# Stick-breaking attention beside HGRN2 on one core: the sum over later keys carried as one row, value products in pairs, a fourth score bank

## The chip, the cores and the metric

One core of a Trainium2 chip runs the whole kernel. The metric is the device time of one execution in microseconds (us). In the rows and in the text the engines are PE (TensorE), DVE (VectorE), ACT (ScalarE), POOL (GpSimd) and SP (SyncE, which issues most transfers). PEld is TensorE's weight load.

## What is computed

One layer of a streaming encoder, for 1024 prompt positions and 8 streams of 16 new positions, all in fp32. After a norm, one projection feeds branch A (stick-breaking attention, 8 heads of 64), branch B (HGRN2, 4 heads of 128) and two merge gates. The change touches branch A's prompt attention:

```python
def stick_breaking_block(q, k, v, q_pos, k_pos):
    z = jnp.einsum('bthd,bshd->bhts', q, k) * (SB_HEAD_DIM ** -0.5)
    mask = k_pos[None, :] < q_pos[:, None]
    log_fail = jnp.where(mask, jax.nn.log_sigmoid(-z), 0.0)
    after = lax.cumsum(log_fail, axis=3, reverse=True) - log_fail
    a = jnp.where(mask, jnp.exp(jax.nn.log_sigmoid(z) + after), 0.0)
    return jnp.einsum('bhts,bshd->bthd', a, v)
...
y = x + rms_norm((merged @ w_out), g_post)
```

With sp = softplus(z), the weight of key s for query t is exp(z - sum of sp over all keys from s up to t). So each key tile needs, besides its own triangle, the sum of sp over all later keys.

## The kernel before

The order of every engine is written out by hand, with semaphores between them. After a prologue (norm, first projections) the program runs four times, once for each pair of heads `p`, an **attention stage** of 27 steps (`B_STEPS`) and then a **recurrence stage** (`A_STEPS`) for HGRN2. Into both stages pieces of eight matmuls of the input projection (`product`, L623) are spread by `B_PIECES` and `A_PIECES`. Then come gates and branch products (L909), the output projection and a tail that normalises and stores y.

An attention step `n` stands for one tile of 128 keys against a window of 512 queries of one head. `STEPS` runs over two windows `wd`, over the key tiles `j` from the last to the first, and over the two heads `h`; `tile_rank(n)` counts the key tiles from the last, and diagonal tiles use only the columns from `first_col(n)` (128, 256, 384 or 512 columns are left). In step n each engine does, in this order:

- PE: the scores of step n into `Z[n % 3]` (L685, L686; the queries split into a high and a low part), pieces of the projection, then for step n-2 the accumulation on the scores (`add`, L699): `negtri` times the softplus's high part SPH and low part SPL, and `negones` times the later-key sum's high part SUH and low part SUL (for the second key tile the fp32 `SUM`, as one fp32 matmul). Then more pieces, and the value product of step n-3 (L739): `v_nat` with 128 columns (both heads' values) against `Aw`, into one bank per head, `OH = (OB, XB)`; half of each result is used.
- ACT: exponential (L1116) and log (L1118) of the scores, together the softplus; the exponential of step n-2's log weights into `Aw` (L1126); evacuations of projection windows (`window_recurrence`, `forget`).
- DVE: the maximum that guards the softplus (L1370), on diagonal tiles the causal product (L1374), SPH and SPL (L1381, L1383), SUH and SUL (L1389, L1391); scans of the forget gate, and the split of the next weight chunk (`split_weights`, L1244, L1246).
- POOL: the causal product on `Aw` (L1678) and the running sum `SUM[h]` (`later_sum`, L1660 to L1670).

The high and low parts are fp32r (a matmul on them is one pass, one on fp32 takes two records). In the tail (L1614, L1619) DVE scales rows 0 to 5 of y and adds the residual, and POOL does rows 6 and 7 (`finish`, L1724, L1726), for each of three windows.

## Time and profile before

| what | us |
|---|---|
| median of 3 runs | 1159.33 (1159.21 to 1160.43) |
| profiled execution | 1159.81 |
| its span, first to last instruction | 1158.0 |
| TensorE busy | 1109.8 |
| VectorE busy | 739.9 |
| ScalarE busy | 466.6 |
| GpSimd busy | 278.6 |

The mean granted clock of TensorE was 0.991 of full speed. Busy times are unions of the records of an engine. A matmul's record is longer than the time that it keeps the array from the next one, since matmuls are pipelined; the distance between the starts of two neighbours tells the second. The attention stages run from 88.5 to 175.8 us, 263.2 to 350.5, 438.0 to 525.3 and 612.7 to 700.0; the recurrence stages lie between them and the last after them.

### The profile page before, as it was taken

The numbers are of one execution on the slowest core, as the hardware profiler recorded it, in microseconds if no ns is written. First come the engines' busy times: TensorE is split into PE (matmuls) and PEld (weight loads), VectorE is DVE, ScalarE is ACT, GpSimd is POOL, SyncE is SP. The second block draws the span as 40 slices with busy tenths as digits, with TensorE's granted clock in tenths as the row PEclk, the third lists the DMA queues.
The fourth block names the chain that finished last, engine by engine and source line by source line (L and its number), as shares of the span: only waits on it lengthen the run. The fifth ranks groups of instructions, "written<-read, shape, count | busy, mean of one in ns | idle before, by whom it ended". The sixth has DMA issues, their size and how long they took to land.

```text
span 1158.0 us, 17212 instructions
## 1 busy us (share of the span) xinstructions
PE 1109.8 (96%) x6486; PEld 1039.7 (90%) x6486; DVE 739.9 (64%) x1347; ACT 466.6 (40%) x923; POOL 278.6 (24%) x306
## 2 busy tenths in 40 slices
PE   3999999999999999999999999999999999999994
PEld 2899988999988999988999987999999999999993
DVE  7747986787986787986787995764332312352228
ACT  4345544155544155543146545346022232242221
POOL 2113422213422213422114422110211100121225
PEclk9999999999999999999999999999999999999997
DMA  6023021115021115021115021205111111111144
GB/s 241 19 71 117 19 91 55 39 46 164 19 92 55 40 39 171 20 91 55 39 40 171 19 91 55 101 19 179 56 37 37 54 39 37 43 49 37 38 182 163
DMA packets 41458, 84.89 MB, mean 73 GB/s; under 512 B 2080, under 2 KB 22176, under 8 KB 41248
## 3 DMA queue, kind: packets, MB, share of 16 engines
q1 hardware_dynamic: 40800, 81.43, 21.6%
q10 hardware_dynamic: 576, 2.36, 0.6%
q8 instruction: 52, 0.85, 0.3%
q14 instruction: 30, 0.25, 0.1%
HBM read 67.27 MB, written 16.52 MB: 72 GB/s over the span
## 4 chain that ended last, share of the span: by engine, by line
PE 88%; DVE 6%; ACT 2%; DMA 1%; issue 1%; SPq 0%; DVEq 0%; ACTq 0%
PE bank L623 56%; PE bank L909 9%; PE bank L699 5%; PE bank L739 5%; PE bank L832 2%; PE bank L855 2%; PE bank L686 2%; PE bank L685 2%; DVE xw L1344 1%; DVE imaskL L1303 1%; DVE yb L1614 1%; PE bank L873 1%; PE bank L783 1%; PE bank L761 1%; DVE St L1530 1%
## 5 line engine op out<-in xcount | busy, mean ns | idle before, releaser
L623 PE MATMUL bank<-xl,wh 128*128 128x384 f32 x1344 | 459.0, 342 | 6.7 <-DVE xl L1340 6.7
L623 PE MATMUL bank<-xh,wh 128*128 128x384 f32 x1344 | 454.9, 338 | 4.3 <-ACT xh L1090 3.5
L623 PE MATMUL bank<-xh,wl 128*128 128x384 f32 x1344 | 456.7, 340 | 0.0
L623 PEld LDWEIGHTS bank<-xl,wh 128*128 128x128 f32 x1344 | 253.5, 189 | 14.3 <-DVE xl L1340 8.1
L623 PEld LDWEIGHTS bank<-xh,wh 128*128 128x128 f32 x1344 | 253.8, 189 | 13.5 <-issue 10.6
L623 PEld LDWEIGHTS bank<-xh,wl 128*128 128x128 f32 x1344 | 253.9, 189 | 7.9 <-issue 4.2
L1244 DVE CAST wh<-wr 128x1024 fp32r<-128x1024 f32 x64 | 51.1, 798 | 102.3 <-PE bank L623 102.3
L1034 ACT ACTIVATE slot<-bank,ngate 128x384 f32<-128x384 f32 x48 | 27.7, 578 | 190.7 <-PE bank L623 188.0
L1701 POOL TENSOR_TENSOR imaskH<-i_nat,k 128x512 fp32r<-128x512 f32 (+1 forms) x36 | 50.5, 1407 | 188.1 <-PE bank L832 188.1
L1246 DVE TENSOR_TENSOR wl<-wr,wh 128x1024 fp32r<-128x1024 f32 x64 | 93.1, 1454 | 2.2
L1713 POOL TENSOR_TENSOR slot<-slot,slot 128x384 f32<-128x384 f32 x24 | 32.7, 1364 | 241.0 <-DVE slot L1579 240.8
L1116 ACT ACTIVATE E<-bank 128x512 f32<-128x512 f32 (+3 forms) x96 | 46.9, 489 | 96.6 <-PE bank L686 96.4
L739 PE MATMUL bank<-Aw,v_nat 128*128 128x512 f32 (+3 forms) x192 | 77.4, 484 | 0.0
L1578 DVE TENSOR_TENSOR slot<-bank,slot 128x384 f32<-128x384 f32 x24 | 13.4, 557 | 100.2 <-PE bank L909 100.2
L1670 POOL TENSOR_TENSOR SUM<-SUM,E 128x512 f32<-128x512 f32 (+3 forms) x64 | 60.2, 941 | 60.5 <-DVE SUL L1391 43.8
L1370 DVE SCALAR_TENSOR_TENSOR E<-E,bank 128x512 f32<-128x512 f32 (+3 forms) x96 | 52.6, 548 | 33.9 <-ACT E L1118 33.8
L909 PE MATMUL bank<-gl,wh 128*128 128x384 f32 x192 | 65.0, 339 | 0.0
L909 PE MATMUL bank<-gh,wh 128*128 128x384 f32 x192 | 65.0, 339 | 0.0
L909 PE MATMUL bank<-gh,wl 128*128 128x384 f32 x192 | 65.0, 339 | 0.0
L1126 ACT ACTIVATE Aw<-bank 128x512 f32<-128x512 f32 (+3 forms) x96 | 46.2, 481 | 42.3 <-PE bank L699 42.3
L1530 DVE SCALAR_TENSOR_TENSOR St<-St,gg,bank 128x128 f32<-128x128 f32 x128 | 44.3, 346 | 23.6 <-PE bank L855 15.8
L1303 DVE SCALAR_TENSOR_TENSOR imaskL<-i_nat,k,imaskH 128x128 fp32r<-128x128 f32 x160 | 53.5, 397 | 0.0
(193 smaller groups left out, 1749.1 us busy)
## 6 DMA issues: line engine op xcount, KB each, us to landing
wr<-wch SPq DMA_DIRECT2D x64, 512.0 KB, 3.7
KTc<-ckT SPq DMA_DIRECT2D x4, 2048.0 KB, 8.9
Vc<-cv SPq DMA_DIRECT2D x4, 2048.0 KB, 8.3
xw<-xT SPq DMA_DIRECT2D x6, 768.0 KB, 10.1
graw<-gated SPq DMA_DIRECT2D x8, 576.0 KB, 5.8
xres<-xT SPq DMA_DIRECT2D x1, 4608.0 KB, 16.6
yT<-yb SPq DMA_DIRECT2D x6, 576.0 KB, 3.0
okT<-kT ACTq DMA_DIRECT2D x4, 576.0 KB, 3.0
```

The source lines that it names most:

```text
L623: i = nc.tensor.matmul(CH[n % 2][:, 0:WIN], weights[:, k, :], rows[:, k, w * WIN:(w + 1) * WIN], start=(m == 0), stop=(m == 23))
L699: return nc.tensor.matmul(Z[m % 3][:, lo:QW], weights, rows[:, lo:QW], start=False, stop=True, skip_group_check=True)
L739: nc.tensor.matmul(OH[h][:, c0:QW], v_nat[:, j * P:(j + 1) * P], Aw[m % 2][:, c0:QW], start=(j == 4 * wd + 3), stop=(j == 0), skip_group_c ...
L909: i = nc.tensor.matmul(bk[:, 0:WIN], weights[:, t, :], rows[:, ROW_OF[t], w * WIN:(w + 1) * WIN], start=(m == 0), stop=(m == 11))
L1116: nc.scalar.activation(E[n % 3][:, c0:QW], Z[n % 3][:, c0:QW], ACT.Exp).then_inc(s_E, 1)
L1244: V.tensor_copy(wh[g % 2][:, :, :], wr[g % 3][:, :, :]).then_inc(s_whi, 1)
L1246: V.tensor_tensor(wl[g % 3][:, :, :], wr[g % 3][:, :, :], wh[g % 2][:, :, :].bitcast(F32), ALU.subtract).then_inc(s_wlo, 1)
L1303: i = V.scalar_tensor_tensor(imaskL[:, b0 + b, :], i_nat[:, c * P:(c + 1) * P], rows[:, b:b + 1], imaskH[:, b0 + b, :].bitcast(F32), ALU.m ...
L1370: i = V.scalar_tensor_tensor(e[:, c0:QW], e[:, c0:QW], 88.0, Z[n % 3][:, c0:QW], ALU.min, ALU.max)
L1530: V.scalar_tensor_tensor(St[(n + 1) % 8][:, :], St[n % 8][:, :], gg[:, n:n + 1], Z[b % 2][:, s * P:(s + 1) * P], ALU.mult, ALU.add).then_i ...
L1670: G.tensor_tensor(dst[:, lo:QW], dst[:, lo:QW], src[:, lo:QW], ALU.add).then_inc(s_S, 1)
L1701: G.tensor_tensor(imaskH[:, b0:b0 + blocks, :], i_nat[:, None, c * P:(c + 1) * P].broadcast_to([P, blocks, P]), rows[:, :, None].broadcast ...
```

## The change

1. **Later-key sums as one row.** `SUM`, `SUH`, `SUL` and POOL's `later_sum` go. Row 0 of the finished log weights of a tile less row 0 of its scores is minus the sum of softplus over that tile and all later keys. ACT copies row 0 of the scores to `zr`; after the accumulation DVE subtracts (`later_row`), ACT writes the high part to row 0 of `RT[h]`, and DVE the low part to row 32 (`later_row_low`). One matmul with `rows_r` (ones in rows 0 and 32) spreads both.
2. **Paired value products.** In every even step PE multiplies the tiles of both heads, each with its own 64 columns of `v_nat`, into partitions 0 to 63 and 64 to 127 of the one bank `OB`.
3. **Fourth score bank.** The bank that is freed joins the score banks (`ZB`). `E` has two buffers and not three, `Aw` three and not two.
4. **High parts by ScalarE.** SPH is written by ACT, after DVE's maximum and before DVE's low part.
5. **Tail.** DVE does all eight rows of y, in three groups for each window; POOL's `finish` goes.

```diff
+def row_col(n):
+    return min(first_col(n), QW // 2)
...
-                        need(pe, s_a, t - 2)
+                        need(pe, s_a, t - 3)
+                        if n >= 4:
+                            need(pe, s_S, SUMS * p + sums_until(n - 4))
...
-                            if q == 1:
-                                pe.wait_ge(s_S, SUMS * p + sums_until(m - 2))
-                                add(negones, SUM[h], cs)
-                            else:
-                                pe.wait_ge(s_Sh, SUM_SPLITS * p + sum_rows_until(m))
-                                add(negones_r[:, :], SUH[h], cs)
-                                pe.wait_ge(s_Sl, SUM_SPLITS * p + sum_rows_until(m))
-                                add(negones_r[:, :], SUL[h], cs)
+                            pe.wait_ge(s_Sl, SUMS * p + sums_until(m - 2))
+                            add(rows_r[:, :], RT[h], row_col(m - 2))
...
-                        nc.tensor.matmul(OH[h][:, c0:QW], v_nat[:, j * P:(j + 1) * P], Aw[m % 2][:, c0:QW],
-                                         start=(j == 4 * wd + 3), stop=(j == 0), skip_group_check=True).then_inc(s_av, 1)
+                        for h in range(2):
+                            r = slice(DH * h, DH * h + DH)
+                            nc.tensor.matmul(OB[r, c0:QW], v_nat[:, j * P + DH * h:j * P + DH * h + DH],
+                                             Aw[(n - 4 + h) % 3][:, c0:QW], start=(j == 4 * wd + 3), stop=(j == 0),
+                                             skip_group_check=True).then_inc(s_av, 1)
...
+                        if STEPS[n][1] > 0:
+                            need(act, s_Sl, SUMS * p + (sums_until(n - 4) if n >= 4 else 0))
+                            nc.scalar.activation(zr[n % 4][0:1, row_col(n):QW], ZB[n % 4][0:1, row_col(n):QW], ACT.Copy)
...
+                    if n < NS and tile_rank(n) > 0:
+                        c0, t = first_col(n), NS * p + n
+                        act.wait_ge(s_sp, t + 1)
+                        nc.scalar.activation(SPH[n % 2][:, c0:QW], E[n % 2][:, c0:QW], ACT.Copy).then_inc(s_sph, 1)
+                    if 2 <= n <= NS + 1 and STEPS[n - 2][1] > 0:
+                        m, cols = n - 2, slice(row_col(n - 2), QW)
+                        act.wait_ge(s_rz, 2 * (p + 1))
+                        act.wait_ge(s_S, SUMS * p + sums_until(m))
+                        nc.scalar.activation(RT[STEPS[m][2]][0:1, cols], zr[m % 4][0:1, cols], ACT.Copy).then_inc(s_Sh, 1)
...
+            def later_row(p, m):
+                cols = slice(row_col(m), QW)
+                row = zr[m % 4][0:1, cols]
+                dve.wait_ge(s_a, NS * p + m + 1)
+                V.tensor_tensor(row, ZB[m % 4][0:1, cols], row, ALU.subtract).then_inc(s_S, 1)
+
+            def later_row_low(p, m):
+                h, cols = STEPS[m][2], slice(row_col(m), QW)
+                dve.wait_ge(s_Sh, SUMS * p + sums_until(m))
+                V.tensor_tensor(RT[h][32:33, cols], zr[m % 4][0:1, cols], RT[h][0:1, cols].bitcast(F32),
+                                ALU.subtract).then_inc(s_Sl, 1)
```

How the order changes. First PE, first attention stage, around a value product of a full-width step. `bank4` holds the scores of step n-2, `k2` and `negtri_r` are constants. Before:

```order
L739 MATMUL bank7<-Aw1_116,v_nat_68 128x512
L685 MATMUL bank3<-QS1_88,KS1_86 128x512
L686 MATMUL bank3<-QL1_81,KS1_86 128x512
L699 MATMUL bank4<-SPH1_106,negtri_r_96 128x512
L699 MATMUL bank4<-SUH1_112,negones_r_97 128x512
L699 MATMUL bank4<-SUL1_114,negones_r_97 128x512
L699 MATMUL bank4<-SPL1_108,negtri_r_96 128x512
```

Now:

```order
L733 MATMUL bank5<-Aw2_116,v_nat_68 64x512
L733 MATMUL bank5<-Aw0_114,v_nat_68 64x512
L689 MATMUL bank7<-QS1_88,KS1_86 128x512
L690 MATMUL bank7<-QL1_81,KS1_86 128x512
L703 MATMUL bank3<-SPH1_105,negtri_r_96 128x512
L703 MATMUL bank3<-RT1_109,rows_r_97 128x512
L703 MATMUL bank3<-SPL1_107,negtri_r_96 128x512
```

Two products of 64 output columns stand in a row, in every second step, where one of 128 stood in each; four accumulations are three.

ACT in one full-width step of the same stage (`bank4` and `bank2` are the scores, `zr` and `RT` the rows). Before:

```order
L1116 ACTIVATE E1_103<-bank3 128x512
L1118 ACTIVATE E1_103<-E1_103 128x512
L1126 ACTIVATE Aw0_115<-bank4 128x512
L944 ACTIVATE tmpT0_94<-bank0 128x384
L1116 ACTIVATE E2_104<-bank4 128x512
```

Now:

```order
L1113 ACTIVATE E0_102<-bank4 128x512
L1116 ACTIVATE zr2_112<-bank4 1x512
L1118 ACTIVATE E0_102<-E0_102 128x512
L1126 ACTIVATE Aw1_115<-bank2 128x512
L1130 ACTIVATE SPH0_104<-E0_102 128x512
L1135 ACTIVATE RT0_108<-zr0_110 1x512
L939 ACTIVATE tmpT1_95<-bank1 128x384
L1113 ACTIVATE E1_103<-bank7 128x512
```

Three instructions of a step are six, and the window's evacuation stands behind the two that wait for DVE.

DVE in the same place. Before:

```order
L1370 SCALAR_TENSOR_TENSOR E0_102<-E0_102,bank2 128x512
L1381 CAST SPH0_105<-E0_102 128x512
L1383 TENSOR_TENSOR SPL0_107<-E0_102,SPH0_105 128x512
L1389 CAST SUH0_111<-SUM0_109 128x512
L1391 TENSOR_TENSOR SUL0_113<-SUM0_109,SUH0_111 128x512
L1423 SCALAR_TENSOR_TENSOR lf_74<-k2_89,lf_74 128x128
```

Now, with the split of a weight chunk behind it:

```order
L1399 SCALAR_TENSOR_TENSOR E0_102<-E0_102,bank4 128x512
L1312 TENSOR_TENSOR zr0_110<-bank2,zr0_110 1x512
L1411 TENSOR_TENSOR SPL0_106<-E0_102,SPH0_104 128x512
L1318 TENSOR_TENSOR RT0_108<-zr0_110,RT0_108 1x512
L1442 SCALAR_TENSOR_TENSOR lf_74<-k2_89,lf_74 128x128
L1253 CAST wh0_57<-wr2_55 128x1024
L1255 TENSOR_TENSOR wl2_56<-wr2_55,wh0_57 128x1024
L1399 SCALAR_TENSOR_TENSOR E1_103<-E1_103,bank7 128x512
```

The casts left DVE; two instructions on one row came in their place, each between two of ACT's.

## Rows read from the trace of the kernel before

**Rows 1.** The page's busy times, and the chain that ended last, by line.

```profile
PE 1109.8 (96%) x6486; PEld 1039.7 (90%) x6486; DVE 739.9 (64%) x1347; ACT 466.6 (40%) x923; POOL 278.6 (24%) x306
...
by line: PE bank L623 55.8%; PE bank L909 8.8%; PE bank L699 5.5%; PE bank L739 5.4%; PE bank L832 2.1%; PE bank L855 1.8%; PE bank L686 1.5%; PE bank L685 1.5%; issue 1.3%; DVE xw L1344 1.2%; DVE imaskL L1303 1.1%; DVE yb L1614 0.7%; PE ba
```

**Rows 2.** Windows of attention stages: length; busy PE, PEld, DVE, ACT, POOL; clock; DMA.

```profile
263.20:350.50 87.30, 87.30 (x462) 77.06 (x464) 72.59 (x145) 46.36 (x97) 29.58 (x48) 1.00 0.27 81
...
sum 349.20, PE 349.20 PEld 308.26 DVE 290.26 ACT 185.48 POOL 118.23; mean PE 87.30 PEld 77.06 DVE 72.57 ACT 46.37 POOL 29.56
```

**Rows 3.** Groups by form, PE, whole span: line, operands, count, busy us, mean ns.

```profile
L699 PE MATMUL bank<-SUL,negones_r 128*128 128x512 f32 x32 | 12.7, 397 | 0.0
...
L761 PE MATMUL bank<-KTc,qbd 128*32 128x512 f32 x64 | 7.7, 598 | 0.0
...
L699 PE MATMUL bank<-SUM,k 128*128 128x128 f32 x32 | 6.1, 274 | 0.0
...
L699 PE MATMUL bank<-SUL,negones_r 128*128 128x384 f32 x16 | 5.4, 340 | 0.0
...
L699 PE MATMUL bank<-SUL,negones_r 128*128 128x256 f32 x16 | 4.4, 278 | 0.0
```

**Rows 4.** Timeline, PE, a full-width step: start us, duration us, line, operands.

```profile
333.29 0.40 PE L699 MATMUL bank<-SUH,negones_r 128*128 128x512 f32 x1
333.52 0.40 PE L699 MATMUL bank<-SUL,negones_r 128*128 128x512 f32 x1
```

**Rows 5.** Timeline, PE, end of the second attention stage: the sample scores.

```profile
349.91 0.61 PE L756 MATMUL bank<-kTs,qbd 128*128 128x128 f32 x4
350.45 1.92 PE L761 MATMUL bank<-KTc,qbd 128*32 128x512 f32 x16
352.30 0.44 PE L623 MATMUL bank<-xh,wh 128*128 128x384 f32 x1
352.58 0.34 PE L623 MATMUL bank<-xl,wh 128*128 128x384 f32 x1
```

**Rows 6.** Timeline, ACT, a full-width step; idle before and its releaser in brackets.

```profile
331.86 0.60 ACT L1116 ACTIVATE E<-bank 128x512 f32<-128x512 f32 x1 [2.24 <-PE bank L686]
332.49 0.63 ACT L1118 ACTIVATE E<-E 128x512 f32<-128x512 f32 x1
334.19 0.60 ACT L1126 ACTIVATE Aw<-bank 128x512 f32<-128x512 f32 x1 [1.07 <-PE bank L699]
334.69 0.49 ACT L959 ACTIVATE tmpT<-bank 128x384 f32<-128x384 f32 x1
335.06 0.50 ACT L944 ACTIVATE zB<-bank 128x384 f32<-128x384 f32 x1
```

**Rows 7.** Groups by form, ACT: copies of other shapes (last row: stage of 264:351).

```profile
L997 ACT ACTIVATE QS<-qT 64x1024 fp32r<-64x1024 f32 x16 | 16.9, 1059 | 0.4
...
L1056 ACT ACTIVATE gh<-graw 128x1152 fp32r<-128x1152 f32 x8 | 9.2, 1156 | 3.3 <-DMA graw<-gated 3.3
...
L1116 ACT ACTIVATE E<-bank 128x256 f32<-128x256 f32 x4 | 1.5, 384 | 3.9 <-PE bank L686 3.9
```

**Rows 8.** Timeline, DVE: a weight split before a maximum; the causal product (ns min/median/max).

```profile
336.73 1.46 DVE L1244 CAST wh<-wr 128x1024 fp32r<-128x1024 f32 x1
338.22 1.23 DVE L1246 TENSOR_TENSOR wl<-wr,wh 128x1024 fp32r<-128x1024 f32 x1
339.37 0.68 DVE L1370 SCALAR_TENSOR_TENSOR E<-E,bank 128x512 f32<-128x512 f32 x1
...
L1374 DVE TENSOR_TENSOR E<-E,k x64: 291/336/907, 86.6 to 654.2; 128x128 f32<-128x128 f32 x64
```

**Rows 9.** Timeline, the tail: second and third window on DVE, POOL and ACT.

```profile
1136.55 1.36 DVE L1614 TENSOR_TENSOR yb<-yb,yrs 128x1152 f32<-128x1152 f32 x1 [1.09 <-ACT yrs L1220]
1136.60 3.00 POOL L1724 TENSOR_TENSOR yb<-yb,yrs 128x768 f32<-128x768 f32 x1 [0.26 <-ACT yrs L1220]
1137.94 2.87 DVE L1619 TENSOR_TENSOR yb<-yb,xres 128x1152 f32<-128x1152 f32 x1
...
1142.14 0.52 ACT L1220 ACTIVATE yrs<-yrs 128x384 f32<-128x384 f32 x1
...
1152.14 1.36 DVE L1619 TENSOR_TENSOR yb<-yb,xres 128x1152 f32<-128x1152 f32 x1
```

177 lines of the change are left out of this document (67 added, 110 removed).

## The prediction

> **What bounds the kernel now.** I began with the chain that ended last and the busy times of the page [rows 1]. The chain is TensorE for 88% of the span, and its two attention lines are 5.4% (L739, the value products) and 5.5% (L699, the accumulations on the scores). So what TensorE no longer does comes off the end, as long as no other engine is late. Then I cut the span into the four attention stages, one for each pair of heads [rows 2]. Each takes 87.3 us, and TensorE is busy for the whole of it; VectorE has 72.6 us of work in it, ScalarE 46.4 and GpSimd 29.6. Beyond these stages the edit touches only the last 20 us, where the output is scaled and the residual is added [rows 9]. The recurrence stages, the gates and the output projection keep their instructions.
>
> **What TensorE loses.** (1) *Later-key sums.* Each of the 64 SUL matmuls goes. In the timeline one of 512 columns follows the next after 0.23 us [rows 4]; with 0.17 for 384 and 0.115 for 256 columns, in proportion, 32, 16 and 16 of them [rows 3] are 7.4 + 2.8 + 1.8 = 12.0 us. The SUH matmul stays as one with RT, with the same columns. The 16 fp32 SUM matmuls of 128 columns are 32 records. A record's duration is its stream and about 0.17 of pipeline (a 512-column one shows 0.40 and is followed after 0.23), so one streams for 0.11, in all 3.4 us. In their place come 16 matmuls of 256 columns at 0.115, 1.8 us. Net 13.6 us over four stages, 3.4 each.
>
> (2) *Value products.* L739 holds 5.4% of 1158.0 us, 62.5 us [rows 1]. Now two products of 64 output columns each, one for each half of the array, stand where two of 128 stood. Does the array run both at once? The sample scores (L761) are the nearest row: products of 32 output columns with 512-column fp32 streams. A record shows 0.60 [rows 3], a stream of 0.43, and 16 of them are done in 1.92 us [rows 5]; one after the other they would take 6.9, so four ran at a time. I take two at a time here: 31.3 us remain.
>
> The same rows show a price. L756's last record ends at 350.52, so its stream ended 0.17 earlier, at 350.35, and L761 is first seen at 350.45. The second of the full-array matmuls behind starts at 352.58; less one spacing of 0.17 the first took effect at 352.41. Between 350.35 and 352.41 lie 2.06 us, and four rounds of 0.43 fill 1.71 of them. So one excursion into divided columns costs 0.35 us. The change makes one every second step, 12 per stage and 48 in all: 16.8 us. Value products then cost 31.3 + 16.8 = 48.1 us and save 14.4, which is 3.6 per stage and not 7.8. The bounds are 0 (the gap at L761 is its weight loads and hides here) and 0.5 us per excursion.
>
> The Trainium skill (TensorEngine Tiling (Array Packing), Key Properties) says that changing the tiling mode drains TensorE; the rows agree. The same skill's tensor-engine page (TensorE: Matmul & The Clock Gate, Measured speedup vs the span model) gives a packed group one matmul's duration and about 4 ns per tile, with no term for the drain; by it alone the sum would be 16.8 us lower.
>
> Together a stage of TensorE's work shrinks from 87.3 to 87.3 - 3.4 - 3.6 = **80.3 us**.
>
> **What the other engines get.** *ScalarE.* Per stage it takes over 20 high parts of the softplus (12 of 512 columns, 4 of 384, 4 of 256), and gets 20 one-row copies zr and 20 one-row copies RT (8 of 512, 4 of 384, 8 of 256 each). One row has no precedent in the trace. The nearest are the copies on 64 partitions, 1.06 us for 1024 columns, beside 1.16 for 1152 on all 128 [rows 7]: the columns count, not the partitions. I take the full price; the lower bound is the cost of a short instruction, half of it. An instruction that waits for nothing follows the last one after 0.50 us at 512 columns and 0.37 at 384 [rows 6], and 0.28 at 256 (0.38 less the same overlap of 0.10) [rows 7]. High parts: 6.0 + 1.5 + 1.1 = 8.6. Each kind of row copy: 4.0 + 1.5 + 2.2 = 7.7. ScalarE: 46.4 + 8.6 + 15.4 = 70.4 us.
>
> It also waits inside the step now, since the high part stands behind VectorE's maximum. That takes 0.68 [rows 8] from the log's end, of which the weights' exponential hides about 0.5: 0.2 us, 20 times. On the 12 diagonal steps with a high part the causal product adds 0.29 [rows 8]. That is 4.0 + 3.5, so ScalarE's own pace is near **78 us per stage**, 2.3 under TensorE's. Queued behind its two new waits are the next step's exponential and the window evacuations, and TensorE waits for both.
>
> *VectorE.* It loses 20 SPH, 16 SUH and 16 SUL instructions per stage and gets 20 + 20 row instructions: much the same total, so I cost it at nothing. The cover is that VectorE is busy for 72.6 us of a stage that still lasts over 80. *GpSimd* loses its sums (L1660 to L1670), and VectorE loses whatever sharing with them costs it.
>
> *Stalls.* The two paces lie close, and the work isn't even. In steps with a 512-column row ScalarE needs about 0.5 + 0.5 + 0.5 + 0.5 for its first four instructions, 0.2 of waiting, and 0.5 + 0.5 for high part and row: 3.3 to 3.5 us. Window work comes on top (30 instructions of about 0.5 in 27 steps, 0.6 per step): 4.1 us. TensorE's mean for such a step is two passes of scores, three accumulations (5 x 0.23), 1.5 pieces of eight at 0.17 (2.1), and half a value pair (0.6): 3.85. Over ten such steps ScalarE falls 2 to 3 us behind. The accumulation of step n comes two steps after its scores, and the fourth score bank lets TensorE run ahead, so about one step (4 us) of lag is hidden. I charge 1.5 us of stall per stage, between 0 and 4. The fourth bank and the third Aw buffer themselves cost nothing.
>
> *The tail.* In the last stage the VectorE instructions take 1.36 us alone and 2.9 beside GpSimd's [rows 9]. Afterwards GpSimd has none and VectorE has six per window: 4 x 1.36 + 2 x 0.91 = 7.3 us. From 1136.55 two windows end at 1151.2, and the third window's rstd (1142.66) is ready before. Before, the last instruction ended at 1153.50. Gain **2.3 us** (1.5 to 3). In the prologue two small fills replace a cast, at most 0.2 us, left out.
>
> **The sum.** 4 x (7.0 - 1.5) = 22.0, and 2.3 at the tail: 24.3 us. The profiled execution took 1159.8 (span 1158.0), 0.5 above the median, which I leave inside the rounding: 1159.8 - 24.3 = **1135.5 us**.
>
> **Rivals.**
> - *A, the exchange between ScalarE and VectorE sets the pace.* For: 46.4 becomes 78 against 80.3, and every step now passes ScalarE, VectorE, ScalarE, VectorE twice. Against: ScalarE idles 2.24 us before a step's first exponential now [rows 6]. If each of 24 steps takes 0.25 us more than I gave it, the stage is 84: 1159.8 - 13.2 - 2.3 = 1144.3 us; with 0.33, 86 and 1152.3.
> - *B, the excursion is free.* TensorE would need 76.1 us per stage, and then ScalarE's 78 sets it: 1159.8 - 37.2 - 2.3 = 1120.3 us. Against it stands the gap in [rows 5]. By the tensor-engine page's rule TensorE would get there, and ScalarE would still hold it at this time.
> - *C, the two halves run one after the other.* Value products 62.5 + 16.8: the stage is 87.3 - 3.4 + 4.2 = 88.1, and the time 1159.8 + 3.2 - 2.3 = 1160.7, no change. Against: four at a time in [rows 5].
> - *D, slower: the weight split blocks the exchange.* In VectorE's queue the split of the next chunk (1.46 + 1.23, 2.7 us) stands ahead of the next step's maximum [rows 8], behind which ScalarE's high part now waits. There are four per stage, 10.8 us. If all of it is exposed on top of 78, the stage is 88.8 and the time 1159.8 + 6.0 - 2.3 = 1163.5. It is slower from 9.9 us exposed (a stage over 87.9). Against: ScalarE's first three instructions of the step, 1.6 us, run beside it, and the lag of a step hides more.
> - *E, it doesn't do what it says:* if rows of one partition went at half price ScalarE would have slack, and my stalls would be 0: 1129.5, inside the forecast.
>
> **Chances.** Forecast (1127 to 1141) 0.51; A (1141 to 1156) 0.21; B (1116 to 1127) 0.13; C 0.05; D 0.10. The range 1120 to 1152 takes in nearly all of A and B; C, D and 0.04 of their outer ends are left out. Faster by over 0.2% (under 1157, about what a measurement of this kernel can tell from no change) 0.85, within 0.2% 0.05, slower 0.10.
>
> **What would show it.** The attention stages: about 82 us each, with TensorE at 80 busy. The spacing at the value pair: two records at a time, and a 0.35 us gap around them; no gap is B, four records in a row is C. The one-row copies at 0.6 us for 512 columns. ScalarE near 71 us busy per stage, its idle before the high part ended by VectorE, and TensorE's idle before L703 ended by VectorE's low parts: 1.5 us per stage is the forecast, over 3 is A, and if it follows weight splits D. Tail: no VectorE instruction over 1.4 us once GpSimd is done. I am wrong if TensorE's work per stage isn't within 79 to 82, or if stalls exceed 4 us.

## The result

| | median us | runs | ratio to before, 95% interval |
|---|---|---|---|
| before | 1159.88 | 1159.21 to 1160.60 | 1 |
| after | 1151.29 | 1150.96 to 1152.38 | 0.9927 [0.9910, 0.9945] |

The change makes the kernel faster by 8.6 us, 0.7%. The forecast was 24.3. The profiled execution has a span of 1150.6 us. Its page, first the busy times and then the chain that ended last, by engine and by line:

```profile
PE 1092.2 (95%) x6406; PEld 1003.2 (87%) x6406; DVE 717.0 (62%) x1307; ACT 556.1 (48%) x1163; POOL 188.6 (16%) x180
...
PE 73%; DVE 12%; ACT 10%; issue 3%; DMA 1%; SPq 0%; ACTq 0%; DVEq 0%
PE bank L621 48%; PE bank L904 9%; DVE E L1399 3%; PE bank L703 2%; PE bank L827 2%; ACT E L1118 2%; PE bank L733 2%; ACT SPH L1130 2%; PE bank L850 2%; ACT E L1113 2%; DVE E L1403 1%; DVE xw L1371 1%; DVE imaskL L1326 1%; PE bank L689 1%; ACT RT L1135 1%
```

Against [rows 1] the chain has left TensorE: its share was 88% and is 73%. In its place stand VectorE's maximum and causal product (L1399, L1403) and ScalarE's exponential, logarithm, high part and row copy (L1113, L1118, L1130, L1135). These are the links of one step's exchange.

The windows of the attention stages, with the columns of [rows 2]:

```profile
262.00:348.60 86.60, 83.32 (x440) 68.29 (x442) 67.73 (x131) 68.75 (x157) 11.46 (x18) 0.98 0.25 82
610.00:696.50 86.50, 82.74 (x444) 67.15 (x446) 67.75 (x131) 68.95 (x158) 11.76 (x19) 1.00 0.26 83
sum 345.60, PE 331.79 PEld 271.04 DVE 270.92 ACT 274.81 POOL 46.08; mean PE 82.95 PEld 67.76 DVE 67.73 ACT 68.70 POOL 11.52
```

TensorE is no longer busy for the whole of a window. Counted from the first score matmul to the first sample score (the **stage length** from here on; the windows above begin about 5 us later), a stage takes 89.98, 90.82, 90.88 and 90.35 us; it took 91.5 before. So a stage gave back about 1 us, not 5.5. What TensorE waited for between 88 and 697 us, the three longest in total (us in total, times, longest):

```profile
PE bank L631 <- ACT tmpT L939: 9.9, 6, 2.3
PE bank L763 <- DVE Es L1304: 4.5, 6, 1.2
PE bank L689 <- DVE zr L1312: 2.4, 8, 0.4
```

And what ScalarE and VectorE waited for there:

```profile
ACT SPH L1130 <- DVE E L1403: 35.3, 48, 0.9
...
ACT SPH L1130 <- DVE E L1399: 19.0, 32, 1.4
...
DVE E L1399 <- ACT E L1118: 45.7, 60, 1.3
...
DVE SPL L1411 <- ACT SPH L1130: 10.5, 48, 0.3
```

L763 waits at the start of the sample attention and did so before. The other two are new. The longest waits are those of the transposes (L631) for an evacuation of a projection window (`tmpT`), which stands in ScalarE's queue behind the high part and the row copy. For the row itself (L703, for VectorE's low part) TensorE waited 0.6 us in all, where the forecast had looked for the stalls.

Where the lag comes from is seen in ScalarE's timeline of step 14, one of the last diagonal steps (start us, duration, line; in brackets the idle time before it and who ended it):

```profile
126.15 0.57 ACT L1113 ACTIVATE E<-bank 128x512 f32<-128x512 f32 x1
126.62 0.57 ACT L1116 ACTIVATE zr<-bank 1x512 f32<-1x512 f32 x1
127.10 0.61 ACT L1118 ACTIVATE E<-E 128x512 f32<-128x512 f32 x1
127.62 0.47 ACT L1126 ACTIVATE Aw<-bank 128x384 f32<-128x384 f32 x1
128.81 0.63 ACT L1130 ACTIVATE SPH<-E 128x512 fp32r<-128x512 f32 x1 [0.72 <-DVE E L1403]
129.34 0.51 ACT L1135 ACTIVATE RT<-zr 1x384 fp32r<-1x384 f32 x1
129.76 0.47 ACT L1004 ACTIVATE kb<-bank 128x384 f32<-128x384 f32 x1
130.13 0.57 ACT L1113 ACTIVATE E<-bank 128x512 f32<-128x512 f32 x1
```

Apart from the 0.72 us in which VectorE takes the maximum and the causal product, ScalarE has no gap: the step takes it 3.98 us. TensorE is quicker there. Its scores of step 12 start at 116.67 us and ScalarE's exponential of them at 118.58; for step 16 it is 129.38 and 135.36. So over four steps TensorE went on by 3.2 us a step and ScalarE by 4.2, and its distance grew from 1.9 to 6.0 us. Two of these four steps, 12 and 15, also hold the three instructions of the forget gate (1.6 us together), so the gate's work is clumped just where TensorE's steps are short. The lag comes out at the transposes of the next steps.

The tail, VectorE in the last window:

```profile
1144.50 1.36 DVE L1638 TENSOR_TENSOR yb<-yb,xres 128x1152 f32<-128x1152 f32 x1
1145.78 0.95 DVE L1633 TENSOR_TENSOR yb<-yb,yrs 128x768 f32<-128x768 f32 x1
```

The 2.87 us of [rows 9] are 1.36 now that GpSimd does nothing there.

### The profile page after: what moved, and what is told of

The parts are those of the page before. It is cut to its first block, busy times and chain, and to the rows that moved or that the text cites. A ratio compares the mean times of both kernels' runs of the same rounds, so it can differ in the third digit from the quotient of the medians.

```text
span 1150.6 us, 17088 instructions
## 1 busy us (share of the span) xinstructions
PE 1092.2 (95%) x6406; PEld 1003.2 (87%) x6406; DVE 717.0 (62%) x1307; ACT 556.1 (48%) x1163; POOL 188.6 (16%) x180
## 4 chain that ended last, share of the span: by engine, by line
PE 73%; DVE 12%; ACT 10%; issue 3%; DMA 1%; SPq 0%; ACTq 0%; DVEq 0%
PE bank L621 48%; PE bank L904 9%; DVE E L1399 3%; PE bank L703 2%; PE bank L827 2%; ACT E L1118 2%; PE bank L733 2%; ACT SPH L1130 2%; PE bank L850 2%; ACT E L1113 2%; DVE E L1403 1%; DVE xw L1371 1%; DVE imaskL L1326 1%; PE bank L689 1%; ACT RT L1135 1%
## 5 line engine op out<-in xcount | busy, mean ns | idle before, releaser
L621 PE MATMUL bank<-xl,wh 128*128 128x384 f32 x1344 | 457.1, 340 | 6.8 <-DVE xl L1367 6.8
L621 PE MATMUL bank<-xh,wh 128*128 128x384 f32 x1344 | 455.7, 339 | 5.3 <-ACT xh L1085 3.7
L621 PE MATMUL bank<-xh,wl 128*128 128x384 f32 x1344 | 457.9, 341 | 0.0
L621 PEld LDWEIGHTS bank<-xh,wh 128*128 128x128 f32 x1344 | 254.6, 189 | 14.4 <-issue 11.6
L621 PEld LDWEIGHTS bank<-xl,wh 128*128 128x128 f32 x1344 | 254.2, 189 | 12.6 <-DVE xl L1367 8.3
L621 PEld LDWEIGHTS bank<-xh,wl 128*128 128x128 f32 x1344 | 254.5, 189 | 6.0 <-issue 2.3
L1253 DVE CAST wh<-wr 128x1024 fp32r<-128x1024 f32 x64 | 43.5, 680 | 102.3 <-PE bank L621 102.3
L1255 DVE TENSOR_TENSOR wl<-wr,wh 128x1024 fp32r<-128x1024 f32 x64 | 95.7, 1496 | 2.2
L1399 DVE SCALAR_TENSOR_TENSOR E<-E,bank 128x512 f32<-128x512 f32 (+3 forms) x96 | 53.0, 552 | 48.9 <-ACT E L1118 48.7
L1597 DVE TENSOR_TENSOR slot<-bank,slot 128x384 f32<-128x384 f32 x24 | 13.4, 557 | 100.2 <-PE bank L904 100.2
L1130 ACT ACTIVATE SPH<-E 128x512 fp32r<-128x512 f32 (+2 forms) x80 | 45.4, 567 | 54.4 <-DVE E L1403 35.3
L1677 POOL TENSOR_TENSOR Aw<-Aw,k 128x128 f32<-128x128 f32 x64 | 35.1, 549 | 184.2 <-ACT Aw L1126 184.2
L1411 DVE TENSOR_TENSOR SPL<-E,SPH 128x512 fp32r<-128x512 f32 (+2 forms) x80 | 49.0, 612 | 13.9 <-ACT SPH L1130 10.5
L1118 ACT ACTIVATE E<-E 128x512 f32<-128x512 f32 (+3 forms) x96 | 49.0, 510 | 0.5
```

What stands on the lines that cost most here:

```text
L621: i = nc.tensor.matmul(CH[n % 2][:, 0:WIN], weights[:, k, :], rows[:, k, w * WIN:(w + 1) * WIN], start=(m == 0), stop=(m == 23))
L1118: nc.scalar.activation(E[n % 2][:, c0:QW], E[n % 2][:, c0:QW], ACT.Ln, bias=1.0).then_inc(s_L, 1)
L1130: nc.scalar.activation(SPH[n % 2][:, c0:QW], E[n % 2][:, c0:QW], ACT.Copy).then_inc(s_sph, 1)
L1253: V.tensor_copy(wh[g % 2][:, :, :], wr[g % 3][:, :, :]).then_inc(s_whi, 1)
L1255: V.tensor_tensor(wl[g % 3][:, :, :], wr[g % 3][:, :, :], wh[g % 2][:, :, :].bitcast(F32), ALU.subtract).then_inc(s_wlo, 1)
L1399: i = V.scalar_tensor_tensor(e[:, c0:QW], e[:, c0:QW], 88.0, ZB[n % 4][:, c0:QW], ALU.min, ALU.max)
```

## Experiments

The runs were made on several chips, each beside runs of the kernel before. So differences are taken between ratios and multiplied by 1159.9 us; with the intervals shown, such a difference is good to about 2 to 5 us. Where that is too coarse I give the stage length of the profiled execution beside it. All kernels (e13, e14, e17 and e18 leave the sum over later keys out of the computation):

| run | what it is | median us | ratio, 95% interval |
|---|---|---|---|
| e1 | before + pairs | 1161.16 | 1.0016 [1.0002, 1.0029] |
| e2 | before + tail | 1153.94 | 0.9953 [0.9939, 0.9966] |
| e6 | before + pairs + fourth bank | 1145.63 | 0.9874 [0.9859, 0.9889] |
| e7 | e6 + tail | 1140.96 | 0.9833 [0.9816, 0.9849] |
| e9 | e7 + high parts by ScalarE | 1148.64 | 0.9913 [0.9888, 0.9938] |
| e4 | after, high parts by VectorE | 1176.47 | 1.0148 [1.0123, 1.0172] |
| e13 | after, row steps left out | 1129.39 | 0.9715 [0.9687, 0.9744] |
| e14 | e4, row steps left out | 1130.07 | 0.9716 [0.9682, 0.9750] |
| e17 | after, row steps without chain | 1149.13 | 0.9914 [0.9893, 0.9935] |
| e18 | e17, VectorE's two only | 1128.71 | 0.9738 [0.9722, 0.9754] |
| e3 | after, turns later | 1148.86 | 0.9905 [0.9884, 0.9926] |
| e5 | after, row high part by GpSimd | 1150.84 | 0.9920 [0.9905, 0.9935] |
| e8 | e5 + e3 | 1153.10 | 0.9936 [0.9921, 0.9950] |
| e10 | after, row high part a step later | 1193.86 | 1.0298 [1.0268, 1.0329] |
| e11 | e10 + e3 | 1192.88 | 1.0294 [1.0269, 1.0318] |
| e12 | after, products moved | 1145.61 | 0.9882 [0.9855, 0.9910] |
| e15 | e12 + e3 | 1146.36 | 0.9865 [0.9836, 0.9893] |
| e16 | e12 + e5 | 1141.23 | 0.9818 [0.9790, 0.9847] |

### Value pairs, banks and tail, one at a time

e1 makes only the value products in pairs, with three score banks:

```diff
-                        nc.tensor.matmul(OH[h][:, c0:QW], v_nat[:, j * P:(j + 1) * P], Aw[m % 2][:, c0:QW],
...
+                        for h in range(2):
+                            r = slice(DH * h, DH * h + DH)
+                            nc.tensor.matmul(OB[r, c0:QW], v_nat[:, j * P + DH * h:j * P + DH * h + DH],
+                                             Aw[(n - 4 + h) % 3][:, c0:QW], start=(j == 4 * wd + 3), stop=(j == 0),
+                                             skip_group_check=True).then_inc(s_av, 1)
```

> The kernel before with the paired value products alone (three Aw buffers, two E buffers to make room; sums, high parts and tail as before). Theory: TensorE loses 62.5/2 us and pays 48 excursions of 0.35 us, so 14.4 us less work, and with ScalarE at 46 us per stage nothing stalls: 1159.9 - 14.4 = 1145.5 us. Rival (the excursion costs what the pairing saves): 1158 to 1160. Rival (excursion free): 1128.7.

No gain: it is rather 1.9 us slower. TensorE's new wait in this kernel:

```profile
PE bank L685 <- ACT Aw L1127: 14.8, 16, 1.2
```

The scores of step n wait for the exponential that frees one of three banks. Before, a value product stood between in every step and covered that; in pairs it is gone from every second one. The time alone would also fit the rival that the excursions eat what the pairing saves, or that two `E` buffers are too few. e6 keeps the pairs and the two buffers and adds the fourth bank:

```diff
-        OH = (OB, XB)
+        ZB = (*Z, XB)
...
-                        need(pe, s_a, t - 2)
+                        need(pe, s_a, t - 3)
```

> The kernel before with paired value products and the fourth score bank (old sums, high parts on VectorE, old tail). Theory (in the pair alone the scores of every second step waited for a bank, and the value product no longer hid that wait): the 3.7 us of waits on the exponential per stage go, and the pairing brings its 14.4 us less the small rest: 1158.6 - 14 = 1144 to 1146 us. Rival (two E buffers or the excursions are what cost the pair alone its gain): 1157 to 1161 again.

The wait is gone, both rivals with it, and the time is 14.6 us under before; the forecast for the pairs was 14.4. The stage length falls from 91.5 to 88.6 us, 2.9 a stage where 3.6 were forecast, so the pairs' sum was right to within about 3 us and the match of 14.6 and 14.4 is closer than the measurement. And "the fourth bank costs nothing" hid that without it the pairs bring nothing.

e2 changes only the tail:

```diff
-                for lo, hi in ((0, 3), (3, 6)):
+                for i, (lo, hi) in enumerate(Y_ROWS):
...
-            finish(0)
```

> The kernel before with the new tail alone. By the two traces the tail gave 4.1 us (2.4 in VectorE, 1.7 behind its last instruction): 1155.8 us. Rival (my sum, VectorE alone, 2.3 us): 1157.6. If the tail of the changed kernel only looks shorter because something ahead moved: 1159.9.

The medians give 4.7 us, the ratio 5.5. e7 puts it on top of e6:

> The same with the new tail. Theory: the two are independent, 4.6 us more: 1140 us, which is faster than the changed kernel although the one-row sums and ScalarE's high parts are left out. Rival: the tail's gain overlaps with nothing else, or the old sums' stalls eat it: 1145 or more.

4.8 us by the ratios, as expected (4.6). e7 is already 10.9 us faster than the changed kernel, which only adds the one-row sums and ScalarE's high parts to it. TensorE does less in the changed kernel, and yet it is slower. From here on this is the question.

### The high parts by the one engine or the other

e4 gives the high parts back to VectorE. My theory then was that ScalarE has too much work:

```diff
+                            V.tensor_copy(SPH[n % 2][:, c0:QW], e[:, c0:QW]).then_inc(s_sph, 1)
...
-                        nc.scalar.activation(SPH[n % 2][:, c0:QW], E[n % 2][:, c0:QW], ACT.Copy).then_inc(s_sph, 1)
```

> The changed kernel with the softplus's high part written by VectorE again, between its maximum and its row step. Theory (ScalarE's queue, with its wait for the maximum, lags): it loses 8.6 us of work and some 13 us of waits per stage, TensorE's stalls of 6 us per stage shrink to under 1: 1151.3 - 21 = 1130 us. Rival (the stalls come from VectorE's side of the row exchange): 1150 to 1156, since VectorE gets 9 us per stage more.

That theory fell, and the rival's 1150 to 1156 was too low as well: 25.6 us slower than after, though ScalarE is rid of 80 instructions (8.6 us in a stage by the prediction's price). ScalarE in this kernel:

```profile
ACT RT L1131 <- DVE zr L1308: 125.7, 80, 2.4
...
326.23 0.57 ACT L1126 ACTIVATE Aw<-bank 128x512 f32<-128x512 f32 x1
329.24 0.63 ACT L1131 ACTIVATE RT<-zr 1x512 fp32r<-1x512 f32 x1 [2.43 <-DVE zr L1308]
```

The row copy RT waits for VectorE's maximum, high part and row in turn, and ScalarE's next exponential stands behind it. The mean of these waits is 1.57 us; the one shown is the longest, since a weight split (L1251, to 327.50) held up the maximum as well. So less work on ScalarE made it worse. What counts here is how long the turns ScalarE, VectorE, ScalarE inside a step take, with all that stands in both queues between them.

e9 is the other corner: e7 with only the high parts moved to ScalarE:

```diff
-                            V.tensor_copy(SPH[n % 2][:, c0:QW], e[:, c0:QW]).then_inc(s_sph, 1)
...
+                        act.wait_ge(s_sp, t + 1)
+                        nc.scalar.activation(SPH[n % 2][:, c0:QW], E[n % 2][:, c0:QW], ACT.Copy).then_inc(s_sph, 1)
```

> The fourth run of a square: the kernel before with paired value products, the fourth score bank and the even tail (1140.96 us) and, on top of it, only the high part of softplus cast by ScalarE between VectorE's steps; the later-key sums stay full tiles on GpSimd and VectorE. The other corners are 1140.96 (neither), 1176.47 (one-row sums alone, all high parts of softplus by VectorE) and 1151.29 (both). Theory: the wait of ScalarE for the maximum costs nothing by itself where ScalarE has only 49 us of work in 86.6 and the cast leaves VectorE, which is the fuller engine (73.9 us of 86.6): 1138 to 1142 us, so that the whole loss of the changed kernel is the one row's. Rival: the exchange ScalarE, VectorE, ScalarE inside a step is itself what takes the time: 1147 us or more.

The rival holds: 9.3 us slower than e7. Without the row step between maximum and low part VectorE waits for the cast each time:

```profile
DVE SPL L1387 <- ACT SPH L1133: 50.8, 80, 0.7
```

and its high and low parts of the full-tile sum stand behind. ScalarE in its turn waits 85.8 us for the maximum, 26.1 of them in the 12 steps in which a weight split runs first (the longest 3.8). So each of the two edits costs when made alone (the high parts 9.3, the one row 36.5 us over e7), and together 10.9.

### Leaving the row steps out, and keeping only their slots

e13 leaves out `zr`, `later_row`, `RT` and `later_row_low`, and TensorE adds a row tile of zeros; e14 is the same with VectorE's casts.

```diff
-                        later_row(p, n - 2)
...
-                        later_row_low(p, n - 2)
...
-                            pe.wait_ge(s_Sl, SUMS * p + sums_until(m - 2))
+                            pe.wait_ge(s_rz, 2 * (p + 1))
```

> The changed kernel without the four steps of the one row (the copy of the bank's first row, its difference, its high and its low part); TensorE still adds the row tile, which holds zeros, so what is left out of the computation is the sum over later keys. TensorE's own work is that of the changed kernel (84.05 us in an attention stage). Theory: the row's steps make 3 to 4 of the 6.5 us of stalls and the exchange through softplus's high part the rest, as in the run that changed only that (stalls 2.9 us): stage 86.9 us, 1135 to 1139 us. Rival: the exchange alone makes them and the row's steps fit beside it: 1147 us or more.

> As the run before, with the high part of softplus cast by VectorE behind its maximum instead of by ScalarE. Theory: without the row's steps VectorE has 1.3 us less in each step than where it took 1176.47 us, and the stalls are the 1.5 us of the paired kernel with four banks and full-tile sums: stage 85.6 us, 1128 to 1133 us, below the run before. Rival: at TensorE's shorter work the chain of a step sets the pace wherever the cast stands: the same as the run before within 2 us, or above it.

e13 is 6 us below what its theory gave. e14 is in its theory's range, but not below e13: the rival was right in that the two are the same. Against e7 they are 13.6 us faster; TensorE's work for the full-tile sums was forecast at 13.6. (The stage length falls from 88.6 to 84.7 us in both, 15.7 over four stages. e14 differs from e7 also in VectorE's and GpSimd's work for the sums, so up to 2 us of this can be small waits that e7 still had.) So all that was to be had from TensorE is there, wherever the high parts are cast: 91.5 to 84.7 is 6.8 us a stage, and 7.0 were forecast. The four row steps cost 0.9927 - 0.9715, or 24.6 us; by the stage lengths, 84.7 against 90.5, it is 23.3. e17 tells slots from chain:

```diff
-                        act.wait_ge(s_S, SUMS * p + sums_until(m))
-                        nc.scalar.activation(RT[STEPS[m][2]][0:1, cols], zr[m % 4][0:1, cols], ACT.Copy).then_inc(s_Sh, 1)
+                        nc.scalar.activation(zr[m % 2][0:1, cols].bitcast(F32R), zr[m % 2][0:1, cols], ACT.Copy).then_inc(s_Sh, 1)
...
-                dve.wait_ge(s_a, NS * p + m + 1)
-                V.tensor_tensor(row, ZB[m % 4][0:1, cols], row, ALU.subtract).then_inc(s_S, 1)
+                row = zr[2 + m % 2][32:33, cols]
+                V.tensor_tensor(zr[2 + m % 2][0:1, cols], row, row, ALU.subtract).then_inc(s_S, 1)
```

> The changed kernel with the row's four steps kept at their places in the queues, with their operations, engines and sizes, but made of rows of their own: ScalarE's copy of the bank's first row goes to a tile that only ScalarE uses, its second copy stays in that tile, VectorE's two differences are of a zero row of its own, and nobody waits for any of the four; TensorE adds a row tile of zeros. What is left out of the computation is the sum over later keys. VectorE's first difference reads SBUF instead of the bank. Theory: the slots cost the time, since ScalarE's copy stands between exp(bank) and the logarithm and the other three stand in front of the next step's exponential and maximum: 1145 us or more. Rival: the chain through the exponential, the row and TensorE's addition costs it: 1129 to 1134 us. Between these, each takes the share that its distance shows.

Nobody waits for the four instructions, and the time is still that of the changed kernel, within the intervals. The slots, that is the places in the queues, cost it. e18 takes ScalarE's two away (lines against e17):

```diff
-                            nc.scalar.activation(zr[n % 2][0:1, row_col(n):QW], ZB[n % 4][0:1, row_col(n):QW], ACT.Copy)
...
-                        nc.scalar.activation(zr[m % 2][0:1, cols].bitcast(F32R), zr[m % 2][0:1, cols], ACT.Copy).then_inc(s_Sh, 1)
```

> As the run before, without ScalarE's two copies: VectorE's two differences of its own zero row stay at their places in its queue (two of 0.67 us a step), and nothing waits for them. The sum over later keys is left out of the computation. Theory: a step's circle is ScalarE's exponential, copy and logarithm, VectorE's maximum, ScalarE's cast and second copy, and VectorE's differences lie beside it: 1129 to 1134 us, so that ScalarE's two copies carry the cost. Rival: the cost is VectorE's, whose differences delay the next maximum: 1143 us or more. Between these both carry a share, as their distances show.

Decided: ScalarE's two copies cost 0.9914 - 0.9738, 20.4 us. VectorE's two come to 0.9738 - 0.9715, 2.7 us, and the chain to 1.5 us; neither is clear of the intervals. The stage lengths of the four stages together say the same: 338.7 us in e13, 340.4 in e18, 362.0 in e17 and 362.0 in the changed kernel, so 1.7 us for VectorE's slots, 21.6 for ScalarE's and nothing for the chain. The same 20.5 us of the first stage, where the lag builds up, in the changed kernel, in e17 and in e18 (columns as in [rows 2]; the stage begins at 83.67, 81.96 and 83.68):

```profile
118.00:138.50 20.50, 18.50 (x99) 15.06 (x97) 13.35 (x31) 17.20 (x39) 2.30 (x5) 1.00 0.09 27
```

```profile
118.00:138.50 20.50, 16.73 (x87) 14.20 (x86) 14.77 (x32) 17.23 (x38) 2.28 (x5) 0.96 0.08 27
```

```profile
118.00:138.50 20.50, 20.50 (x114) 18.03 (x113) 17.32 (x35) 14.40 (x30) 3.18 (x6) 1.00 0.09 27
```

With the copies ScalarE is busy for 17.2 of 20.5 us, and the rest is its waits for VectorE's maximum: its time is full, and TensorE's is not. Without them it does 30 instructions in 14.4 us and TensorE is busy for the whole stretch. VectorE does even more there (17.3). A step of e18 on ScalarE, the one that answers to the step shown above:

```profile
123.42 0.58 ACT L1111 ACTIVATE E<-bank 128x512 f32<-128x512 f32 x1
124.03 0.63 ACT L1113 ACTIVATE E<-E 128x512 f32<-128x512 f32 x1
124.57 0.47 ACT L1121 ACTIVATE Aw<-bank 128x384 f32<-128x384 f32 x1
125.76 0.63 ACT L1125 ACTIVATE SPH<-E 128x512 fp32r<-128x512 f32 x1 [0.72 <-DVE E L1392]
126.30 0.47 ACT L1002 ACTIVATE kb<-bank 128x384 f32<-128x384 f32 x1
126.67 0.59 ACT L1111 ACTIVATE E<-bank 128x512 f32<-128x512 f32 x1
```

3.25 us from exponential to exponential, not 3.98. ScalarE falls behind in e18 too (its distance grows from 1.3 to 3.9 us over steps 12 to 16), but TensorE hardly waits for it (0.7 us in all at the transposes): the rest of the lag, up to 6.0, is what the copies add and what TensorE meets.

### Can the order hide it?

e3 lets the transposes, and VectorE's copies of their results, come one step later:

```diff
-                    for w12 in late:
+                    for w12 in later:
                         turn_recurrence(p, w12)
-                    late = ended(B_PIECES[n])
+                    later, late = late, ended(B_PIECES[n])
```

> The changed kernel with the transposes of the HGRN2 value windows, on TensorE and VectorE, one attention step later. Theory (a local lag of ScalarE of one step, which meets TensorE at these transposes): the 2.6 us wait per stage and the low clock behind it (1.1 us in two stages) go: 1151.3 - 10.4 - 2.2 = 1139 us, or 1141 if the waits on the row remain. Rival (ScalarE's pace over the stage is the bound, the wait only shows it): the time comes back at the next wait, 1149 to 1151.

2.6 us, the rival's side: the waits go from L631 to the scores (L689, 7.7 us) and the row (L703, 4.0 us). So the lag is ScalarE's, and TensorE meets it at the next place.

e5 gives the row's high part to GpSimd, e8 adds e3:

```diff
-                        nc.scalar.activation(RT[STEPS[m][2]][0:1, cols], zr[m % 4][0:1, cols], ACT.Copy).then_inc(s_Sh, 1)
+                        G.tensor_copy(RT[STEPS[m][2]][0:1, cols], zr[m % 4][0:1, cols]).then_inc(s_Sh, 1)
```

> The changed kernel with the row's high part (RT row 0) written by GpSimd and not by ScalarE. Theory (a circle of two engines: ScalarE can't start step n+1 before RT of step n-2, which waits for VectorE's row step, which stands behind the maximum of step n, which waits for ScalarE's log): the circle loses the row step and RT, 3.5 us become 2.9 per full-width step, below TensorE's 4.05, and most of the 6 us of stall per stage goes: 1128 to 1134 us on the clock of the changed kernel's first measurement (1151.3). Rival (ScalarE's amount of work, or the row's latency, is what counts): it loses only 7.7 us of work per stage and gains GpSimd's latency in the row: 1147 to 1152.

> Row's high part on GpSimd, and the transposes of the value windows one step later. Theory of the circle: the transposes don't wait any more with the row on GpSimd, so this changes nothing against the run without it (within 1.5 us). Rival (the lag at the transposes is its own cause, from the forget gate's three instructions): 6 to 10 us faster than the row on GpSimd alone.

Neither gains. One copy less on ScalarE halves the wait for the transposes, but GpSimd takes 1.15 us for a row of 512 columns, and now TensorE waits for the row:

```profile
PE bank L703 <- DVE RT L1313: 8.4, 8, 1.4
PE bank L631 <- ACT tmpT L939: 5.0, 8, 0.9
```

e10 casts the row's high part one step later, between the weights' exponential and the high part of softplus, where ScalarE idles; e11 adds e3:

```diff
-                    if 2 <= n <= NS + 1 and STEPS[n - 2][1] > 0:
-                        m, cols = n - 2, slice(row_col(n - 2), QW)
+                    if 3 <= n and STEPS[n - 3][1] > 0:
+                        m, cols = n - 3, slice(row_col(n - 3), QW)
```

> The changed kernel with the row's high part cast by ScalarE one step later and between exp(bank) and the high part of softplus, so that ScalarE has 0.63 us more to do while VectorE takes the maximum; the low part by VectorE one step later too. Theory: ScalarE's idle time before the high part of softplus (35.3 us in 48 diagonal steps and more in the others over the four stages) is a link of the circle of a step, and the cast now fills it: stalls of TensorE fall from 6.5 us in a stage to 2 to 4, 1135 to 1143 us. Rival: the circle is closed through the row of the same head, which now has one step less of slack: 1151 us or more.

> As the run before, with the transposes of the recurrence one step later too, as in the earlier run that did only that (1148.86 us). Theory: in the changed kernel the transposes' wait only moved the lag of the exchange; where the exchange's lag is gone, the transposes need no slack: within 1.5 us of the run before. Rival: both slacks are needed together: 3 us or more below it.

The idle time is filled, and the kernel is 43 us slower than after, on the rival's side; e11 is the same within 1.5 us. TensorE's new wait in e10:

```profile
PE bank L703 <- DVE RT L1318: 38.9, 38, 2.0
```

My reading, from the order of the queues: the row's low part, one step later, now stands in VectorE's queue behind the softplus's low part of the following step, which waits for ScalarE, and TensorE, which works in order, holds the next scores behind its addition. Measured is only the wait: 38 of the 80 row additions.

e12 moves products from the three last steps, which have no scores, to steps 14 to 19:

```diff
-B_PIECES = spread([700 if n < 2 else max(QW - first_col(n), 300) if n < NS else 400 for n in range(B_STEPS)], 12 * PIECES)
+B_PIECES = spread([700 if n < 2 else max(QW - first_col(n), 300) + (130 if 14 <= n < 20 else 0) if n < NS else 200
+                   for n in range(B_STEPS)], 12 * PIECES)
```

> The changed kernel with the recurrence's products spread differently: three fewer in the three last steps without scores for each stage, one or two more in steps 14 to 19, where TensorE waits most. Nothing else differs. Theory: the stalls of steps 15 to 19 (4.8 of the stage's 6.5 us) are time in which TensorE has too little of its own work beside a ScalarE and VectorE exchange that needs about 4 us a step; work moved there from the end fills them: 3 to 4 us less in a stage, 1137 to 1142 us. Rival: the products bring their own evacuations to ScalarE (0.5 us each) and lengthen the same exchange: 1149 to 1153 us.

5.2 us, between the two expectations, and the most that a change of order alone gave. The transposes' waits fall from 9.9 to 4.3 us:

```profile
PE bank L632 <- ACT tmpT L940: 4.3, 4, 1.1
PE bank L704 <- DVE RT L1319: 3.3, 4, 0.8
```

> The changed kernel with the products moved to steps 14 to 19 (1145.61 us by itself) and the transposes of the recurrence one step later (1148.86 by itself, against 1151.29). In the run with the products moved TensorE still waits 1.2 us at step 16 and 2.6 at step 23, mostly for the transposes' source. Theory: the two fill different waits: 1140 to 1143.5 us. Rival: the wait moves to the exchange, as it did where the transposes alone were moved: 1144.5 us or more.

> The changed kernel with the products moved and the row's high part cast by GpSimd instead of ScalarE (1150.84 us by itself; ScalarE 59.8 us busy in 86.6 there). Theory: if it is the slots in ScalarE's queue that bind at the steps the products were moved to, two changes add up: 1139 to 1143 us. Rival: GpSimd's 1.15 us for a row lengthen the row's chain by what ScalarE gains: 1144.5 to 1148 us.

e15 has the rival's median, with intervals that overlap e12's. e16 holds the theory: together 12.6 us, where e5 and e12 alone sum to 6.0 (with these intervals the difference is hardly clear of noise). Taking a copy off ScalarE seems to pay once more of TensorE's work stands in the full stretch; why is not shown. e16 and e7 are the two fastest kernels that compute the whole; they can't be told apart (0.9818 and 0.9833).

## Why the forecast was off

The parts, by the prediction's own terms, in us of the whole time:

| term | forecast | measured | by |
|---|---|---|---|
| later-key sums off TensorE | -13.6 | -13.6 | e14 against e7 |
| value products in pairs | -14.4 | -14.6 | e6 |
| tail | -2.3 | -4.8 | e7 against e6 |
| stalls | +6.0 | +24.6 | after against e13 |
| sum | -24.3 | -8.4 | after: 0.9927, -8.5 |

The measured rows are steps of one ladder (before, e6, e7, e14 or e13, after), so their sum comes out by construction; what it tests is only that e13 and e14 are the same.

**TensorE's work** was right: the stage length without the row steps is 6.8 us shorter than before, and 7.0 were forecast, so 87.3 becomes 80.5 where 80.3 was meant. (The windows show TensorE busy for 82.95, which is no measure of its work: a record lasts longer than its stream, and some stood at half the clock.) That each part came out within 0.2 us over the whole kernel is luck; by the stage lengths the sums gave 3.9 a stage and not 3.4, the pairs 2.9 and not 3.6. The price of an excursion into divided columns shows in the timeline:

```profile
326.26 0.34 PE L621 MATMUL bank<-xl,wh 128*128 128x384 f32 x1
326.53 1.08 PE L733 MATMUL bank<-Aw,v_nat 128*64 128x512 f32 x4
327.54 0.50 PE L689 MATMUL bank<-QS,KS 128*128 128x512 f32 x1
327.87 0.40 PE L690 MATMUL bank<-QL,KS 128*128 128x512 f32 x1
```

The stream of L621 ends at 326.43, and that of L689 began one spacing of 0.23 before the next, at 327.64. Of the 1.21 us between, two rounds of 0.43 are 0.86, which leaves 0.35, the value read from [rows 5]. By the same reckoning ten of the first stage's twelve excursions cost 0.35 us, at 128 to 512 columns, and the other two 0.40 and 0.42. Rival B falls. C falls too: the four records start in two pairs, each pair within 0.01 us, and all are done in 1.08 us. The rule of the Trainium skill (TensorE: Matmul & The Clock Gate, Measured speedup vs the span model) agrees with this trace in that a pair takes one matmul's time; it has no term for the 0.35 us around it.

**ScalarE's work** was right: 70.4 us forecast, 68.70 measured. One-row copies cost the full price, as much as an instruction on a whole tile; E falls (count, busy us, mean ns):

```profile
L1135 ACT ACTIVATE RT<-zr 1x512 fp32r<-1x512 f32 x32 | 20.2, 631 | 0.6
L1116 ACT ACTIVATE zr<-bank 1x512 f32<-1x512 f32 x32 | 18.3, 571 | 0.0
```

**The stalls were mis-sized**, and this is the step that failed. I put 78 us of ScalarE beside 80.3 of TensorE over a stage, looked for unevenness only among the full-width steps (ScalarE 2 to 3 us behind after ten of them), let one step of lag, 4 us, hide it, and charged 1.5 us a stage. Measured are 6.1 by the ratios and 5.8 by the stage lengths. My own sign for being wrong, stalls over 4 us, is met. Three things were wrong in that.

First, the uneven place is the last diagonal steps. There TensorE's steps are short (3.2 us from step 12 to 16, waits included, and 2.9 in e13), and ScalarE's are not (4.2, and 4.1 over the seven steps behind): the forget gate's instructions come in two of the four, and it waits 0.72 us for the maximum and the causal product, where I had 0.5.

Second, the lag that is hidden isn't that of the scores, for which the fourth bank stands. TensorE meets ScalarE first where the slack is shortest: at the transposes, whose evacuation is queued behind ScalarE's row copy (and, with these a step later in e3, at the scores and the row).

Third, I compared sums over a stage. The two copies are busy for 78.5 us over the four stages (L1116 and L1135, all forms) and cost 20.4 at the end: that they count only where ScalarE has no time left is what the stretch of 20.5 us shows for the first stage. The place to look for it would have been the two engines' work step by step.

What happened is nearest to rival A, whose 0.33 us per step gives 1152.3. But that figure was one of two trial values and its agreement with 1151.29 is no merit, and the exchange sets the pace only in a part of the stage (TensorE still holds 73% of the chain), filled up by ScalarE's copies.

**D** (the weight split) is seen but small: in the 12 steps in which a split runs before the maximum, ScalarE waits 1.12 us before the high part on the mean (13.4 in all, the longest 1.40), where 0.28 is common in a full-width step. It was not tried by itself.

**The tail** gave twice its forecast. I counted VectorE's instructions, and these are as forecast (1.36 us each). What I left out lies behind the last one: the span ends 2.9 us after VectorE's last instruction and not 4.5. The last store carries two rows of y (128x768) now and not three (128x1152), which is my reading of it and was not tried by itself.

**The fourth bank** "costs nothing" was true and beside the point: e1 shows that the pairs are worth nothing without it.

What stays open: why the high parts on ScalarE cost 9.3 us in e9 and nothing in e13. The rows show VectorE's wait in e9, that two full-tile instructions stand behind it, and ScalarE's long waits behind weight splits; which of these is the reason was not tried by itself. Nor was a kernel that leaves out only one of ScalarE's two copies.

## What to carry to other kernels

Work that leaves the bounding engine comes off the end only if the others keep pace at each place, so set the engines' work side by side step by step and not stage by stage, and look for the steps where the bounding engine's work shrinks and the others' does not. An instruction on an engine that has no time left in a step is paid in full, even if it touches one row and nobody waits for it. A part that "costs nothing" should be tried alone as well: without the fourth bank the 14.6 us of the pairs are not there.

## What the runs showed of the hardware

The granted clock fell to half at a wait of 2.33 us. The second stage, from the transposes on, with two windows (clock in the third number from the end) and the rows around it:

```profile
312.60:315.50 2.90, 2.87 (x10) 2.68 (x11) 2.83 (x5) 1.93 (x4) 0.89 (x1) 0.50 0.01 3
315.70:318.00 2.30, 2.30 (x14) 2.16 (x14) 2.16 (x4) 2.06 (x4) 0.00 (x0) 1.00 0.00 0
...
312.63 0.90 PE L631 MATMUL bank<-k,tmpT 128*128 128x128 f32 x3 [2.33 <-ACT tmpT L939]
...
314.50 0.52 PE L621 MATMUL bank<-xh,wl 128*128 128x384 f32 x1
314.82 0.52 PE L621 MATMUL bank<-xh,wh 128*128 128x384 f32 x1
```

The spacing is 0.32 us where it was 0.17, at 1.2 and not 2.4 GHz, for 2.9 us, of which half is lost: a wait of 2.3 us cost up to 1.4 more behind it (an estimate from these rows). The third stage shows the same. In the first stage the same wait was followed by the full clock, and in the fourth too:

```profile
139.38 0.55 PE L631 MATMUL bank<-k,tmpT 128*128 128x128 f32 x3 [2.32 <-ACT tmpT L939]
...
138.50:158.00 19.50, 18.33 (x93) 14.85 (x94) 17.45 (x29) 16.76 (x33) 1.01 (x1) 1.00 0.08 28
```

In e17, where the wait is 2.9 us in each stage, the half clock follows in all four. Why it follows the wait of 2.3 us in two stages and not in the others isn't shown by any run.

VectorE gained within the stages too, where I had charged nothing: it is busy for 67.7 us of a stage and not 72.6. The cast of a weight chunk is the same instruction in both kernels (count, busy us, mean ns), before:

```profile
L1244 DVE CAST wh<-wr 128x1024 fp32r<-128x1024 f32 x64 | 51.1, 798 | 102.3 <-PE bank L623 102.3
```

and after:

```profile
L1253 DVE CAST wh<-wr 128x1024 fp32r<-128x1024 f32 x64 | 43.5, 680 | 102.3 <-PE bank L621 102.3
```

GpSimd has 11.5 us of work in a stage now and had 29.6. That this is the reason was not tried; it fits with the tail, where VectorE's instructions beside GpSimd's took 2.87 us and now take 1.36. What it gave in time here isn't shown.
